# One layer step of a gated hybrid decoder on one core: six edits to a hand-ordered kernel (a bank's own signal, a norm moved, gates from a sum, transposes, constant matmuls, paired outputs)

## The chip, the cores and the metric

The kernel runs on one core of one Trainium2 chip. The metric is device time in microseconds for one launch. A run is also profiled; the profile's span is the time from the first to the last instruction of that execution.

## The reference

One step of one decoder layer in float32, for a prompt of 512 tokens and for 8 samples of one token each, model width 1024. All of it is computed for both.

```
h = rmsnorm(x, g_norm)
a_u, a_v, a_z, b_q, b_k, b_v, b_gd, b_z, c_q, c_z, gl = split(h @ w_in)
# A: spatial gating
vn    = layernorm(gelu(a_v), ln_v_g, ln_v_b)            # also an output, for the samples
out_a = gelu(a_u) * (tril(w_s) @ vn + b_s) * silu(a_z)
# B: gated linear attention, 4 heads, dk 128, dv 256
glog  = log_sigmoid(b_gd @ w_g_up + b_g) / 16            # b_gd = h @ (1024 x 16)
o, S  = chunked (prompt) or S = exp(g) S + k v, o = q S  (each sample, from its own state)
out_b = rmsnorm(o, gn_g) * silu(b_z)
# C: cross attention, 4 heads of 256, over 256 memory tokens
out_c = softmax(c_q k / 16) v * silu(c_z)                # samples: keys and values from a cache
x = x + sum_i(sigmoid(gl_i + b_gate_i) * (out_i @ w_branch_i)) @ w_out ;  y = rmsnorm(x, g_final)
```

## The kernel before

Activations are kept transposed: 128 channels on the partitions, 8 slices `k` of channels, and 520 columns (512 tokens, then the 8 samples). Every projection is an output of 1024 channels, cut in 8 tiles of 128. There are 17 of them, in the order of `NAMES`: QK, K, V, BV, BZ, CQ, GB, AZ, PB, AV, AU, GA, PA, CZ, GC, PC, OUT. A tile is named here by projection and number, AU6 is the seventh of AU.

Float32 accuracy comes from three products of split numbers: a weight `raw` is rounded to `w_hi` by ScalarE (`hi`, line 530), VectorE takes the remainder `w_lo` (`lo`, line 1390), and TensorE adds hi x lo, lo x hi and hi x hi over the 8 slices (`project`, line 1016). A tile is 48 such matmuls of some 260 columns. A pair of tiles is loaded by SP from DRAM to one of two slots of `raw`; the load of a pair waits for `split_done` of the pair two before.

There is no scheduler. Each engine runs a list written by hand: for each projection and each tile `c`, ScalarE does `hi` of the tile after next, the evacuation of the tile's bank in PSUM, and its hooks; VectorE does `lo` of the tile after next, `post`, and its hooks; TensorE does the projection and its hooks. So whatever stands in a hook of VectorE delays the next `lo` behind it.

The places that the change touches:

- **The start.** TensorE runs eight constant products of `ident` and `tri` (line 1315), then the transpose of the parameters (line 1317), and `x_turn` (line 1290), which transposes normalised x. ScalarE writes `h_hi` from the turned bank (line 551), VectorE `h_lo` (line 1821). The first two block columns of QK are made by `first_half` (line 1303).
- **K and V.** Between them TensorE makes the gates' low-rank input from `h_lo` and `h_hi` (line 1343), in four column groups `32 * i`.
- **BV and AV** are `HALVED`: the first 256 tokens are made as rows, two tiles together (line 994, for n = 0 and 1), the rest as columns (line 981). ScalarE's `evac_halves` copies both row banks out (lines 619 and 620) after both are done. `BEHIND` are the projections that follow, BZ and AU; their first tile uses the banks of the first half.
- **GB and AZ.** VectorE updates a sample's state of 4 x 128 x 256 (`sample_state`), one of four slots; POOL stores it and loads the state of the sample four later when `so_done` says that the slot was read. TensorE's `sample_out` (line 1143) multiplies the state with q, four heads in four column groups.
- **AV and AU.** VectorE's `decode_scores` (line 1709) multiplies cached keys with q. In AU, hooks of tiles 2 to 6 hold `layer_norm(n)`: rows 0 to 3 are blocks of 128 tokens in `tok`, row 4 the samples in `stok`. VectorE makes the statistics (lines 1677 and 1678), ScalarE the root (`ln_root`, line 797), VectorE the scaling (line 1681). For the token blocks POOL multiplies with `lng` and adds `lnb` (lines 467 and 468); for the samples VectorE does so (lines 1685 and 1686). The mix (line 1155, at GA's first tile) waits for all of them (`vn_ready`, `vns_ready`). AU's tile is evacuated to `stage` (line 668) and multiplied by VectorE (line 1410).
- **CZ0.** The decode attention's result `o_sb` is brought to channels on partitions by products with a selection `sel`, which POOL builds (line 1194), and copied to `ocs` (line 1528).

## Time and profile before

| | us |
|---|---|
| time of three runs, median (lowest to highest) | 871.77 (871.34 to 872.13) |
| time of the profiled execution | 871.54 |
| its span | 869.8 |
| TensorE matmuls busy | 854.6 (98%) |
| VectorE busy | 423.7 (49%) |
| ScalarE busy | 376.6 (43%) |
| POOL busy | 90.7 (10%) |
| DMA, mean over the span | 145 GB/s |

A row of a timeline gives start, duration, engine, line of the kernel, operation, output and inputs, shape, count, and in brackets how long the engine had been idle before it and what released it. Consecutive equal instructions are merged in one row. A float32 product of TensorE is recorded as two instructions, a transpose as one. `PEld` is the weight load of TensorE. The chain of waits is followed back from the last instruction.

### The profile page before, as it was taken

The page shows a single profiled execution, that of the slowest core. Times are in us where ns is not written, and L with a number is a line of the kernel's source. Part 1 is how long each engine was busy: PE and PEld are TensorE (multiplying, and loading weights), DVE is VectorE, ACT ScalarE, POOL GpSimd, SP SyncE. Part 2 cuts the span into 40 slices and gives each one's busy share as a digit, 9 for nine tenths or more (in the row PEclk, how much of TensorE's full clock was granted, in tenths as well). Part 3 has the DMA queues.
Part 4 walks back from the last instruction along what each step waited for, and adds up shares of the span by engine and source line. Part 5 has one row for each costly group of instructions (what it writes and reads, how often), then busy time and mean ns, then how long its engine had stood idle before and what let it go on. Part 6 is the DMA issues. An engine that isn't in the chain of part 4 may idle for free.

```text
span 869.8 us, 16391 instructions
## 1 busy us (share of the span) xinstructions
PE 854.6 (98%) x6975; PEld 826.9 (95%) x6975; DVE 423.7 (49%) x737; ACT 376.6 (43%) x596; POOL 90.7 (10%) x129
## 2 busy tenths in 40 slices
PE   7999999999999999999999999999999999999997
PEld 6999999999999999999999999999989999999995
DVE  5524542634554466323346778645343544445634
ACT  7534445246665442322232256433234544534424
POOL 1001000000000222101012147000110000000000
PEclk9999999999999999999999999999999999999999
DMA  8325743231322669523466951425563332252402
GB/s 294 80 87 170 250 146 97 93 104 49 97 99 75 217 212 348 175 67 106 164 215 213 323 194 49 148 98 194 194 243 98 97 123 72 98 189 79 145 2 99
DMA packets 86068, 126.11 MB, mean 145 GB/s; under 512 B 3058, under 2 KB 72736, under 8 KB 86000
## 3 DMA queue, kind: packets, MB, share of 16 engines
q1 hardware_dynamic: 72288, 76.58, 27.1%
q0 software_dynamic: 13616, 48.48, 15.7%
q8 instruction: 54, 0.88, 0.4%
q14 instruction: 14, 0.11, 0.0%
q10 hardware_dynamic: 96, 0.06, 0.0%
HBM read 112.91 MB, written 12.19 MB: 144 GB/s over the span
## 4 chain that ended last, share of the span: by engine, by line
PE 95%; DMA 1%; DVE 1%; ACT 1%; issue 1%; POOL 0%; ACTq 0%; DVEq 0%; POOLq 0%; SPq 0%
PE mm L1016 64%; PE mm L981 5%; PE mm L994 4%; PE mm L970 3%; PE mm L1303 2%; PE mm L1228 2%; DMA raw<-in_w_in_dram 1%; PE p L955 1%; PE p L957 1%; PE p L956 1%; PE mm L1249 1%; PE mm L1248 1%; PE mm L1247 1%; PE p L1155 1%; PE p L1185 1%; PE p L1129 1%
## 5 line engine op out<-in xcount | busy, mean ns | idle before, releaser
L1016 PE MATMUL mm<-h_lo,w_hi 128*128 128x260 f32 (+1 forms) x1088 | 223.3, 286 | 1.7 <-ACT tok L620 1.7
L1016 PE MATMUL mm<-h_hi,w_hi 128*128 128x260 f32 (+1 forms) x1088 | 219.0, 283 | 0.0
L1016 PE MATMUL mm<-h_hi,w_lo 128*128 128x260 f32 (+1 forms) x1088 | 218.5, 282 | 0.0
L1390 DVE TENSOR_TENSOR w_lo<-raw,w_hi 128x1024 fp32r<-128x1024 f32 x130 | 158.2, 1220 | 95.1 <-ACT w_hi L530 94.1
L1016 PEld LDWEIGHTS mm<-h_lo,w_hi 128*128 128x128 f32 x1088 | 167.9, 188 | 7.7 <-issue 6.0
L1016 PEld LDWEIGHTS mm<-h_hi,w_hi 128*128 128x128 f32 x1088 | 167.5, 188 | 0.0
L1016 PEld LDWEIGHTS mm<-h_hi,w_lo 128*128 128x128 f32 x1088 | 167.5, 188 | 0.0
L530 ACT ACTIVATE w_hi<-raw 128x1024 fp32r<-128x1024 f32 x130 | 135.9, 1053 | 7.5 <-issue 3.3
L1016 PE MATMUL mm<-x_lo,w_hi 128*128 128x260 f32 (+1 forms) x448 | 96.2, 284 | 0.0
L1016 PE MATMUL mm<-x_hi,w_hi 128*128 128x260 f32 (+1 forms) x448 | 95.3, 283 | 0.0
L1016 PE MATMUL mm<-x_hi,w_lo 128*128 128x260 f32 (+1 forms) x448 | 95.1, 282 | 0.0
L1016 PEld LDWEIGHTS mm<-x_lo,w_hi 128*128 128x128 f32 x448 | 71.2, 188 | 2.6 <-issue 2.6
L1016 PEld LDWEIGHTS mm<-x_hi,w_hi 128*128 128x128 f32 x448 | 71.2, 188 | 0.0
L1016 PEld LDWEIGHTS mm<-x_hi,w_lo 128*128 128x128 f32 x448 | 71.1, 188 | 0.0
L655 ACT ACTIVATE stage<-mm 128x520 f32<-128x520 f32 x24 | 14.5, 605 | 89.3 <-PE mm L1016 89.3
L671 ACT ACTIVATE gate<-mm,prm 128x520 f32<-128x520 f32 x24 | 16.7, 694 | 60.8 <-PE mm L1016 60.5
L994 PE MATMUL mm<-w_hi,h_lo 128*128 128x256 f32 x128 | 36.6, 286 | 0.0
L981 PE MATMUL mm<-h_lo,w_hi 128*128 128x264 f32 x128 | 36.6, 286 | 0.0
L981 PE MATMUL mm<-h_hi,w_lo 128*128 128x264 f32 x128 | 36.3, 283 | 0.0
L981 PE MATMUL mm<-h_hi,w_hi 128*128 128x264 f32 x128 | 36.3, 283 | 0.0
L994 PE MATMUL mm<-w_lo,h_hi 128*128 128x256 f32 x128 | 35.9, 281 | 0.0
L994 PE MATMUL mm<-w_hi,h_hi 128*128 128x256 f32 x128 | 35.9, 281 | 0.0
(358 smaller groups left out, 1361.2 us busy)
## 6 DMA issues: line engine op xcount, KB each, us to landing
raw<-in_w_in_dram SPq DMA_DIRECT2D x44, 1024.0 KB, 5.3
raw<-in_w_branch_dram SPq DMA_DIRECT2D x12, 1024.0 KB, 5.1
raw<-in_w_mem_kv_dram SPq DMA_DIRECT2D x8, 1024.0 KB, 5.6
gate<-in_cache_mem_k_dram POOLq DMA_DIRECT2D x16, 512.0 KB, 6.0
tok<-in_cache_mem_v_dram POOLq DMA_DIRECT2D x14, 512.0 KB, 5.8
tok<-in_state_gla_dram POOLq DMA_DIRECT2D x8, 512.0 KB, 6.8
out_dram<-tok POOLq DMA_DIRECT2D x8, 512.0 KB, 6.4
work<-scr_q POOLq DMA_DIRECT2D x8, 512.0 KB, 4.9
```

The lines of the kernel that those rows point to most:

```text
L530: A(w_hi[:, j], raw[:, j // 2, :, (j % 2) * P:(j % 2 + 1) * P], ACT.Copy).then_inc(hi_ready, 1)
L655: ins = A(st, src, ACT.Copy)
L671: ins = A(out3(gate), src, ACT.Sigmoid, bias=bg1[:, i * KT + c:i * KT + c + 1])
L955: MM(out, w[0], x[1], start=first_mm, stop=False)
L956: MM(out, w[1], x[0], start=False, stop=False)
L970: ins = MM(mm[:, j // 2, n, 0:2 * P], xp[:, k, ns], wp[:, j - 1:j + 1, k, :], start=(k == 0 and xp is x_lo), stop=(k == KT - 1 and xp is x ...
L981: ins = MM(mm[:, j % 2, 0, 0:TT - 256], wp[:, j, k, :], xp[:, k, 256:TT], start=(k == 0 and xp is h_lo), stop=(k == KT - 1 and wp is w_hi ...
L994: ins = MM(mm[:, n, 1, 0:2 * P], xp[:, k, n * P:(n + 1) * P], wp[:, j - 1:j + 1, k, :], start=(k == 0 and xp is h_lo), stop=(k == KT - 1 a ...
L1016: ins = MM(mm[:, j % 2, a, 0:c1 - c0], wp[:, j, k, :], xp[:, k, c0:c1], start=(k == 0 and wp is w_hi and xp is xl), stop=(k == KT - 1 and ...
L1228: ins = MM(o_bank[j % 4][:, 0:TT - 256], wp, xp[:, k, 256:TT], start=(k == 0 and xp is h_lo), stop=(k == KT - 1 and last))
L1303: ins = MM(mm[:, j % 2, j // 2, 0:c1 - c0], wp[:, j, k, :], xp[:, k, c0:c1], start=(k == 0 and xp is h_lo), stop=(k == KT - 1 and wp is w_ ...
L1390: V.tensor_tensor(w_lo[:, j], raw[:, j // 2, :, (j % 2) * P:(j % 2 + 1) * P], f32(w_hi[:, j]), ALU.subtract).then_inc(split_done, 1)
```

## The change

Six edits:

1. In BV and AV, TensorE signals the rows' first bank alone (`rows0_done`), ScalarE copies it out while the second is made and signals `rows0_out`, and the first tile of BZ and AU waits for that and for the first half's evacuation, no longer for the rows' second copy.
2. The samples' norm leaves `layer_norm`. Its statistics and root (`samples_norm`) stand at AU1, scaling, weight and bias (`samples_affine`, now two operations) at AU3, both with scalars of their own.
3. VectorE sums `h_hi` and `h_lo` into `h_sum`, one slice at each tile of K, and the gates are made from the sum, 32 products in place of 64.
4. The decode result is turned by eight transposes with `ident`, and four strided copies pick the columns; `sel` is gone.
5. The eight constant products at the start become twelve, four, two and four products of 128 columns from `state`, which VectorE fills with ones; they stand before and after the parameters' transpose and between the turns of x. The samples' input has a semaphore of its own, and ScalarE's second weight split moves from behind the eighth slice of `h_hi` to behind the sixth.
6. The samples' outputs are made two at a time, at GB4, GB6, AZ0 and AZ2, in place of one at each of GB3 to AZ2.

```diff
@@ evac_halves, ScalarE
+                cs = bass.ds((it * 4 + j - 1) * P, 2 * P)
+                act.wait_ge(sem("rows0_done"), HALVED.index(name) * KT // 2 + 2 * it + j // 2 + 1)
+                A(tok[:, 0, cs], mm[:, 0, 1, 0:2 * P], f).then_inc(sem("rows0_out"), 1)
                 act.wait_ge(prod_done, g + j + 1)
-                cs = bass.ds((it * 4 + j - 1) * P, 2 * P)
-                A(tok[:, 0, cs], mm[:, 0, 1, 0:2 * P], f)
                 A(tok[:, 1, cs], mm[:, 1, 1, 0:2 * P], f).then_inc(evac_done, 1)
@@ project, TensorE
-                wait(pe, evac_done, t if name in BEHIND and t == first(name) else t - 1)
+                wait(pe, evac_done, t - 1)
+                if name in BEHIND and t == first(name):
+                    pe.wait_ge(sem("rows0_out"), (BEHIND.index(name) + 1) * KT // 2)
@@ start and hooks, ScalarE
                 if k == 1:
                     hi(0, 0, 16)
-            hi(1, 1, 16)
+                if k == 5:
+                    hi(1, 1, 16)
...
-            act.wait_ge(sem("start_loaded"), 96)
+            act.wait_ge(sem("stok_loaded"), 16)
...
+                if name == "AU" and c == 1:
+                    act.wait_ge(sem("ln_mv"), 1)
+                    A(slstd, smv[:, 1:2], ACT.Sqrt, bias=eps_col[0:B, :]).then_inc(sem("ln_rt"), 1)
-                if name == "AU" and 2 <= c <= NT + 2:
+                if name == "AU" and 2 <= c < NT + 2:
                     ln_root(c - 2)
@@ hooks, TensorE
-                if name == "GB" and c >= 3:
-                    sample_out(c - 3)
-                if name == "AZ" and c <= 2:
-                    sample_out(c + 5)
+                if name == "GB" and c in (4, 6) or name == "AZ" and c in (0, 2):
+                    b = c - 4 if name == "GB" else c + 4
+                    sample_out(b)
+                    sample_out(b + 1)
@@ decode, TensorE
-                        ins = MM(p67[:, 0, k * B:(k + 1) * B], o_sb[:, k * P:(k + 1) * P], sel[:, k // 2, :, :],
-                                 start=(k == 0), stop=(k == KT - 1), skip_group_check=True)
+                        ins = TRP(p67_8[:, k, :], o_sb[:, k * P:(k + 1) * P], ident[:, :])
@@ start, TensorE
-            pe.wait_ge(sem("tri_ready"), 1)
-            for _ in range(8):
-                MM(mm[:, 0, 1, 0:2 * P], ident[:, :], tri[:, :, :], start=True, stop=True)
-            pe.wait_ge(sem("start_loaded"), 96)
+            def keep_busy(count):
+
+                for _ in range(count):
+                    MM(mm[:, 0, 1, 0:P], state[:, 0, 0:P], state[:, 0, 0:P], start=True, stop=True)
+
+            pe.wait_ge(sem("eps_ready"), 2)
+            keep_busy(12)
+            pe.wait_ge(sem("ident_ready"), 1)
+            pe.wait_ge(sem("start_loaded"), 80)
             TRP(prm_bank, prm_rows, ident[0:46, 0:46]).then_inc(sem("prm_T"), 1)
+            keep_busy(4)
...
                 if k == 4:
+                    keep_busy(2)
                     pe.wait_ge(sem("x_n"), 2)
                 x_turn(X_A + k)
+            keep_busy(4)
@@ gates, TensorE
-                        for xp in (h_lo, h_hi):
-                            for i in range(4):
-                                ins = MM(p67[32 * i:32 * i + RANK, 0, 0:Q4], gd_w[:, k, :], xp[:, k, i * Q4:(i + 1) * Q4].bitcast(F32),
...
+                        pe.wait_ge(sem("h_sum"), k + 1)
+                        for i in range(4):
+                            ins = MM(p67[32 * i:32 * i + RANK, 0, 0:Q4], gd_w[:, k, :], h_sum[:, k, i * Q4:(i + 1) * Q4],
@@ hooks, VectorE
+                if name == "K":
+                    if c == 0:
+                        dve.wait_ge(sem("memT_done"), KT)
+                    V.tensor_tensor(h_sum[:, c, :], f32(h_hi[:, c, :]), f32(h_lo[:, c, :]), ALU.add).then_inc(sem("h_sum"), 1)
...
                     if c == 1:
                         decode_scores((15,))
+                        samples_norm()
...
-                    if 2 <= c <= NT + 2:
+                    if 2 <= c < NT + 2:
                         layer_norm(c - 2)
+                    if c == 3:
+                        samples_affine()
...
-                    V.tensor_copy(ocs[:, :, :], p67[:, 0, 0:KT * B].rearrange("p (k b) -> p k b", b=B)).then_inc(sem("ocs_ready"), 1)
+                    for h in range(CH):
+
+                        turned = p67_8[:, 2 * h:2 * h + 2, :].rearrange("p d (j x) -> p d j x", x=32)[:, :, :, h:h + 8:4]
+                        ins = V.tensor_copy(ocs[:, 2 * h:2 * h + 2, :].rearrange("p d (g j) -> p d j g", j=4), turned)
+                    ins.then_inc(sem("ocs_ready"), 1)
@@ norms, VectorE (layer_norm keeps the token blocks alone)
+            def samples_norm():
+
+                dve.wait_ge(tr_used, TR["AV"] + KT)
+                dve.wait_ge(sem("stok_in"), 2 * KT)
+                for a in range(2):
+                    link(V.bn_stats(stats[0:B, a, :], stok[:, a * 512:(a + 1) * 512]))
+                V.bn_aggr(smv, stats[0:B, :, :]).then_inc(sem("ln_mv"), 1)
+                dve.wait_ge(sem("ln_rt"), 1)
+                link(V.reciprocal(slrst, slstd))
+
+            def samples_affine():
+
+                dve.wait_ge(sem("a_loaded"), 48)
+                link(V.scalar_tensor_tensor(out=stok[:, :], in0=stok[:, :], scalar=smv[:, 0:1], in1=lng[0:B, :],
+                                            op0=ALU.subtract, op1=ALU.mult))
+                V.scalar_tensor_tensor(out=stok[:, :], in0=stok[:, :], scalar=slrst, in1=lnb[0:B, :],
+                                       op0=ALU.mult, op1=ALU.add).then_inc(sem("vns_ready"), 1)
@@ VectorE's list begins
             V.memset(eps_col, EPS).then_inc(sem("eps_ready"), 1)
+            V.memset(state[:, 0, :], 1.0).then_inc(sem("eps_ready"), 1)
```

How the instructions stand at three of these places follows; the line numbers of the changed kernel differ from those of the kernel before. The start of TensorE's list, before:

```order
L1315 MATMUL mm<-tri,ident 128x256 [waits tri_ready,ident_ready]
L1315 MATMUL mm<-tri,ident 128x256 x7
L1317 MATMUL mm<-ident,stage 128x46 [waits start_loaded]
L1290 MATMUL p<-ident,mz 128x128 [waits x_n,x_n_act]
L1290 MATMUL p<-ident,mz 128x128 x7
```

And in the changed kernel:

```order
L1317 MATMUL mm<-state 128x128 [waits eps_ready]
L1317 MATMUL mm<-state 128x128 x11
L1323 MATMUL mm<-ident,stage 128x46 [waits start_loaded,ident_ready]
L1317 MATMUL mm<-state 128x128 x4
L1291 MATMUL p<-ident,mz 128x128 [waits x_n,x_n_act]
L1291 MATMUL p<-ident,mz 128x128 x7
L1317 MATMUL mm<-state 128x128 x2
```

The constants no longer wait for POOL, and there are some on both sides of the parameters' transpose. VectorE's list at AU6, before, from the last token block's norm in AU5 to the two splits at GA's beginning (`w_lo` is the split of a weight, `stok` are the samples' rows):

```order
L1681 TENSOR_SCALAR tok<-tok,small 128x1024 [waits dve_link]
L1390 TENSOR_TENSOR w_lo<-raw,w_hi 128x1024 [waits hi_ready]
L1410 TENSOR_TENSOR t<-t,stage 128x520 [waits evac_done]
L1504 SCALAR_TENSOR_TENSOR state<-p,tri 128x1024 [waits st_stored,wsT_done]
...
L1681 TENSOR_SCALAR stok<-stok,small 8x1024 [waits dve_link]
L1685 TENSOR_TENSOR stok<-stok,work 8x1024 [waits a_loaded,ln_norm]
L1686 TENSOR_TENSOR stok<-stok,work 8x1024 [waits dve_link]
L1390 TENSOR_TENSOR w_lo<-raw,w_hi 128x1024 [waits hi_ready]
```

The same engine in the changed kernel, AU1 and the split after it, and then AU3 and the split after it:

```order
L1705 BN_STATS small<-stok 8x6 [waits stok_in,tr_used]
L1705 BN_STATS small<-stok 8x6 [waits dve_link]
L1706 BN_AGGR small<-small 8x2 [waits dve_link]
L1708 RECIPROCAL small<-small 8x1 [waits ln_rt]
L1399 TENSOR_TENSOR w_lo<-raw,w_hi 128x1024 [waits hi_ready,dve_link]
...
L1698 TENSOR_SCALAR tok<-tok,small 128x1024 [waits dve_link]
L1713 SCALAR_TENSOR_TENSOR stok<-stok,small,work 8x1024 [waits a_loaded]
L1715 SCALAR_TENSOR_TENSOR stok<-stok,small,work 8x1024 [waits dve_link]
L1399 TENSOR_TENSOR w_lo<-raw,w_hi 128x1024 [waits hi_ready]
```

The samples' work stands ahead of the splits of AU4 and AU6 and no longer ahead of that of GA1. VectorE's list in K, before and in the changed kernel, two tiles each:

```order
L1401 COPY tok<-p 128x2x128 [waits tr_done]
L1390 TENSOR_TENSOR w_lo<-raw,w_hi 128x1024 [waits hi_ready]
L1401 COPY tok<-p 128x2x128 [waits tr_done]
L1390 TENSOR_TENSOR w_lo<-raw,w_hi 128x1024 [waits hi_ready]
L1401 COPY tok<-p 128x2x128 [waits tr_done]
```

```order
L1410 COPY tok<-p 128x2x128 [waits tr_done]
L1450 TENSOR_TENSOR gate<-h_hi,h_lo 128x520 [waits memT_done]
L1399 TENSOR_TENSOR w_lo<-raw,w_hi 128x1024 [waits hi_ready]
L1410 COPY tok<-p 128x2x128 [waits tr_done]
L1450 TENSOR_TENSOR gate<-h_hi,h_lo 128x520
```

A sum stands behind each copy, and the next split behind the sum.

## Rows read from the trace of the kernel before

**Rows 1.** The page: busy time, share of the span and instructions of each engine.

```profile
PE 854.6 (98%) x6975; PEld 826.9 (95%) x6975; DVE 423.7 (49%) x737; ACT 376.6 (43%) x596; POOL 90.7 (10%) x129
```

**Rows 2.** Who TensorE waited for: us in total, times, longest us.

```profile
PE mm L1016 <- ACT tok L620: 1.7, 2, 0.8
PE p L1155 <- issue: 1.5, 1, 1.5
```

**Rows 3.** Timeline of the start: start us, us, engine line op.

```profile
2.65 6.49 PE L1315 MATMUL mm<-tri,ident 128*128 128x256 f32 x16 [2.65 <-POOL tri L377]
...
8.02 0.88 DVE L1816 TENSOR_SCALAR mz<-mz,small 128x512 f32<-128x512 f32 x2
...
9.80 0.84 ACT L551 ACTIVATE h_hi<-p,prm 128x256 fp32r<-128x256 f32 x2 [0.22 <-PE p L1290]
...
10.53 1.06 ACT L530 ACTIVATE w_hi<-raw 128x1024 fp32r<-128x1024 f32 x1
...
13.78 1.05 ACT L551 ACTIVATE h_hi<-p,prm 128x256 fp32r<-128x256 f32 x2 [0.74 <-PE p L1290]
...
17.09 0.39 PE L1303 MATMUL mm<-h_lo,w_hi 128*128 128x256 f32 x1 [0.65 <-DVE w_lo L1390]
```

**Rows 4.** SP's two first weight loads, line 322: durations, first and last start, landing.

```profile
L322 SPq DMA_DIRECT2D raw<-in_w_in_dram x2: 427/518/608, 1.7 to 2.9; - x2
...
DMA to landing us min/median/max: 7.6/9.9/12.1
```

**Rows 5.** The chain of waits, in order of time: start us, us, what.

```profile
90.27 3.67 PE p L1343 x128
...
214.84 1.73 PE p L1129 x8
...
300.60 17.27 PE mm L1016 x144
317.87 0.55 PE p L1143 x8
318.42 5.94 PE mm L1016 x48
...
513.41 17.47 PE mm L1016 x144
...
655.03 1.68 PE p L1194 x16
...
665.41 0.87 PE p L1085 x8
```

**Rows 6.** Timeline of VectorE in BV, an operation with two inputs of 128x520.

```profile
166.57 0.68 DVE L1570 TENSOR_TENSOR gate<-gate 128x520 f32<-128x520 f32 x1
```

**Rows 7.** Timeline of VectorE at the end of K.

```profile
86.56 0.43 DVE L1401 COPY tok<-p 128x256 f32<-128x256 f32 x1 [1.51 <-PE p L1027]
...
89.62 0.42 DVE L1401 COPY tok<-p 128x256 f32<-128x256 f32 x1 [1.51 <-PE p L1027]
89.96 1.22 DVE L1390 TENSOR_TENSOR w_lo<-raw,w_hi 128x1024 fp32r<-128x1024 f32 x1
```

**Rows 8.** Timeline of VectorE and POOL in AU.

```profile
507.86 0.70 DVE L1410 TENSOR_TENSOR t<-t,stage 128x520 f32<-128x520 f32 x1 [2.54 <-ACT stage L668]
...
520.28 1.22 DVE L1390 TENSOR_TENSOR w_lo<-raw,w_hi 128x1024 fp32r<-128x1024 f32 x1
...
522.20 2.12 DVE L1410 TENSOR_TENSOR t<-t,stage 128x520 f32<-128x520 f32 x1 [0.69 <-ACT stage L668]
...
527.20 1.23 DVE L1390 TENSOR_TENSOR w_lo<-raw,w_hi 128x1024 fp32r<-128x1024 f32 x1
...
539.23 1.39 DVE L1677 BATCH_NORM_STATS2 small<-stok 8x6 f32<-8x512 f32 x2
...
542.23 1.21 DVE L1685 TENSOR_TENSOR stok<-stok,work 8x1024 f32<-8x1024 f32 x1
...
520.42 3.33 POOL L467 TENSOR_TENSOR tok<-tok,work 128x1024 f32<-128x1024 f32 x1 [0.97 <-DVE tok L1681]
```

More of the change, by code:

```diff
@@ L192, in bass_gated_parallel_step @@
         eps_col = small[:, 70:71]
+        smv, slstd, slrst = small[0:B, 71:73], small[0:B, 73:74], small[0:B, 74:75]
         def piece(base, at, shape):
@@ L209, in bass_gated_parallel_step @@
         Q4 = TT // 4
+        h_sum = gate
         eb = piece(work, 0, (BH, P))
@@ L252, in bass_gated_parallel_step @@
         sc = piece(work, 3744, (MT, B * CH))
-        sel = piece(work, 3808, (CH, 2, 4))
         o_sb = piece(work, 2 * D, (D,))
@@ L436, in _ @@
             pool.memset(pz.rearrange("p m b c -> p (m b c)"), 0.0).then_inc(sem("sel_ready"), 1)
-            link(pool.memset(sel.rearrange("p h g j -> p (h g j)"), 0.0))
-            pool.affine_select(out=sel, in_=sel, compare_op=ALU.not_equal, fill=1.0, base=0,
-                               pattern=[[-1, CH], [-4, 2], [-32, 4]], channel_multiplier=1).then_inc(sem("sel_ready"), 1)
             def load_q(b):
@@ L559, in _ @@
                 act.dma_start(prm_rows[at:at + rows.shape[0], :], rows).then_inc(sem("start_loaded"), 16)
-            act.dma_start(stok[:, :], x_sample.rearrange("b t d -> (b t) d")).then_inc(sem("start_loaded"), 16)
+            act.dma_start(stok[:, :], x_sample.rearrange("b t d -> (b t) d")).then_inc(sem("stok_loaded"), 16)
             act.wait_ge(sem("eps_ready"), 1)
@@ L794, in ln_root @@
             def ln_root(n):
-                rows = P if n < NT else B
-                act.wait_ge(sem("ln_mv"), n + 1)
-                A(lstd[0:rows, :], mv[0:rows, 1:2], ACT.Sqrt, bias=eps_col[0:rows, :]).then_inc(sem("ln_rt"), 1)
+                act.wait_ge(sem("ln_mv"), n + 2)
+                A(lstd, mv[:, 1:2], ACT.Sqrt, bias=eps_col[:, :]).then_inc(sem("ln_rt"), 1)
             def decode_exp():
@@ L995, in project_halves @@
                                      start=(k == 0 and xp is h_lo), stop=(k == KT - 1 and xp is h_hi and wp is w_hi))
+                    if n == 0:
+                        ins.then_inc(sem("rows0_done"), 1)
                 ins.then_inc(prod_done, 1)
@@ L1281, in out_project @@
                 out_rows(1, 1)
-            pe.wait_ge(sem("ident_ready"), 1)
             def x_turn(u):
@@ L1340, in _ @@
                     for k in range(KT):
-                        for xp in (h_lo, h_hi):
-                            for i in range(4):
-                                ins = MM(p67[32 * i:32 * i + RANK, 0, 0:Q4], gd_w[:, k, :], xp[:, k, i * Q4:(i + 1) * Q4].bitcast(F32),
-                                         start=(k == 0 and xp is h_lo), stop=(k == KT - 1 and xp is h_hi), skip_group_check=True)
+                        pe.wait_ge(sem("h_sum"), k + 1)
+                        for i in range(4):
+                            ins = MM(p67[32 * i:32 * i + RANK, 0, 0:Q4], gd_w[:, k, :], h_sum[:, k, i * Q4:(i + 1) * Q4],
+                                     start=(k == 0), stop=(k == KT - 1), skip_group_check=True)
                     ins.then_inc(sem("gd_done"), 1)
@@ L1671, in layer_norm @@
             def layer_norm(n):
[L1672 to L1675 removed]
+                rows = tok[:, n, :]
                 for a in range(2):
[L1677 to L1686 removed]
+                    link(V.bn_stats(stats[:, a, :], rows[:, a * 512:(a + 1) * 512]))
+                V.bn_aggr(mv, stats).then_inc(sem("ln_mv"), 1)
+                dve.wait_ge(sem("ln_rt"), n + 2)
+                link(V.reciprocal(lrst, lstd))
+                V.tensor_scalar(rows, rows, mv[:, 0:1], lrst, ALU.subtract, ALU.mult).then_inc(sem("ln_norm"), 1)
+            def samples_norm():
[12 more added lines that the diff above has]
+                                       op0=ALU.mult, op1=ALU.add).then_inc(sem("vns_ready"), 1)
             def mix(h):
```

15 lines of the change are left out of this document (removed).

## Prediction

> **What bounds the kernel now.** I read the page's busy times first. TensorE is busy for 854.6 of 869.8 us [rows 1], so the end moves only if TensorE gets less work or waits less. Its list of waits comes next: 1.7 us in two waits for the ScalarE copy of line 620, and 1.5 us in one wait before the mixing matmuls of line 1155 [rows 2]. The rest of its idle time lies in the start. Six stretches of the timeline then give the prices. The sum is made against the profiled execution, 871.54 us, which lies 0.23 us under the median of the three runs (871.77); I keep that execution as the base. About 0.2% (1.7 us) is what a measurement of this kernel can tell from no change.
>
> **1. Start.** Before, sixteen constant matmul records (eight fp32 products) keep TensorE until 9.1 us, though the first half of the token block's norm is scaled at 8.02 + 0.44 = 8.5 us (0.88 us is for both halves) [rows 3]. Afterwards the constants need only a short fill of `state` by VectorE, which can be done at about 1.3 us, instead of the triangle at 2.65. Each record takes 6.49 / 16 = 0.41 us for 256 columns, so 0.20 us for 128: 24 records end at about 6.2, the parameters' transpose comes then, and 8 more records end near 8.2. The turns of x start at 8.5 instead of 9.3. The parameters are in place long before, so ScalarE's first `h_hi` moves from 9.80 to about 9.0, and `w_hi` of tile 0 from 10.53 to about 9.7. Its weights were issued at 1.74 and land 7.6 us later, at 9.3 [rows 4], so they just allow this. Gain 0.8 us. Then tile 1: ScalarE idles 0.74 us before its seventh `h_hi` [rows 3]; the second weight split moves into that hole, while `h_hi` and `h_lo` of the last two slices come after it. That brings `w_lo` of tile 1 forward by another 0.5 us, and TensorE waits for exactly that at 17.09 [rows 3]. Together **-1.3 us**. If the constants end late or the weights land late it is 0; at most it is 1.3 plus the remaining 0.65 of idle time, -1.7 with what is hidden behind it. The samples' rows have a semaphore of their own, which only frees a wait that costs nothing today.
>
> **2. Gates from the sum.** The 128 records of line 1343 take 3.67 us [rows 5]; half of them take 1.8. For it VectorE makes eight sums of 128x520 inside K; the same shape, both inputs in SBUF, takes 0.68 us [rows 6]. A K tile takes TensorE 89.62 - 86.56 = 3.06 us by VectorE's copies, and VectorE 0.42 + 1.22 us [rows 7], so 0.68 more fits and the first six sums are covered. The last two are not: VectorE's copy of tile 6 starts at 89.62, the sum follows until 90.7, the next `w_lo` until 91.8, the copy of tile 7 until 92.2, the last sum until 92.9. TensorE, which begins the gates at 90.27, reaches the eighth slice at 91.8 and waits 1.1 us. It ends near 93.1 instead of 93.94: **-0.8 us**, between 0 (the sums are later still) and -1.8 (no wait). What queues behind the sums on VectorE, the splits of V, is next needed ten us later; SP's loads are issued 0.7 us later and still in time.
>
> **3. First bank of BZ and AU.** TensorE waits for that copy twice, before BZ and before AU, 1.7 us together, 0.85 each [rows 2]. Now the first bank is copied out while TensorE makes the second half of the rows, so both waits go: **-0.85 us at BZ** and as much at AU, which I book below.
>
> **4. Paired outputs of the samples.** Three plain tiles take 17.27 us, 5.76 each. With a sample's eight records between them the time from one to the next is 318.42 + 5.94 - 317.87 = 6.49 [rows 5], so an interruption costs 0.73 us. Four of the eight records run beside each other; at 0.216 us per record of 256 columns (1.73 us for eight that don't, line 1129 [rows 5]) the work itself is 2 x 0.216 = 0.43. The other 0.30 is the price of entering and leaving. Eight become four interruptions: 4 x 0.30 = **-1.2 us**. The states of samples 4 and 6 are now reloaded up to 4 us later, since their slots are free a tile later; I see no wait in it because they are used two tiles after that. Bounds: 0 (the gap is per record) and -1.5.
>
> **5. Samples' norm, in AU.** This is where the change can hurt. Removed: the wait of 1.5 us before the mix [rows 2], which VectorE causes by working on `stok` until 542.23 + 2 x 1.21 = 544.7 [rows 8]. Added earlier on VectorE: `samples_norm` after the last decode score (two statistics of 1.39 us together [rows 8], the aggregate, a wait for ScalarE's root, a reciprocal: some 2.2 us), and `samples_affine` behind the norm of the second row block (two operations of 1.21 us [rows 8]). The first falls into the 2.54 us that VectorE waits at 507.86 [rows 8], but ScalarE must load the Sqrt table and then the Gelu table again before it can evacuate AU's third tile, so I let the chain of norms start 0.5 us later. The second has no hole. VectorE's cycle per tile is 527.20 - 520.28 = 6.92 us there against 17.47 / 3 = 5.82 of TensorE [rows 5, 8], so it lives on its lead. And it meets POOL: `t<-t,stage` takes 2.12 us at 522.20 instead of 0.70, ending 0.6 us behind POOL's multiply (520.42 + 3.33 = 523.75); that multiply itself waited for `w_lo` to end [rows 8]. One holds the other up for a whole instruction, some 2.2 us of POOL work each.
> So: first affine operation 520.8 to 522.0. While the second waits for the first's result, POOL's multiply gets in, until 524.2. Second operation to 525.4, `w_lo` of AU6 behind it to 526.6. Before, AU6 began at 513.41 + 2 x 5.82 = 525.05 [rows 5]; with AU's gain of 0.85 it is due at 524.2 and stalls 2.4 us. The tiles behind it stall no more. Sum of this part: -0.85 - 1.5 + 2.45 = **+0.1 us**. Bounds: -2.35 if nothing collides, and +2.2 if POOL's addition also gets in ahead of `w_lo` (2.2 us more).
>
> **6. Decode transposes.** Sixteen records in 1.68 us become eight transposes; eight of these take 0.87 us [rows 5]. **-0.8 us.** The four small copies in place of one end long before VectorE's maximum of the scores, and POOL loses two small operations nobody waits for.
>
> Sum: -1.3 - 0.8 - 0.85 - 1.2 + 0.1 - 0.8 = -4.85; 871.54 - 4.85 = **866.7 us**.
>
> **Rivals.**
> (a) POOL first. At 525.4 both POOL's addition (asked for at 524.3) and `w_lo` want to go. The rows show POOL and VectorE each waiting for the other once, never a queue of two VectorE operations against a waiting POOL [rows 8], so this is nearly as likely as my case. Then `w_lo` of AU6 ends at 528.8, the stall is 4.6 us, part 5 is +2.2 and the time 868.8.
> The Trainium skill (SBUF — State Buffer, Who interferes with whom) says that issue order decides who blocks, and that the one that issued first holds the shared ports for its whole instruction. The 2.12 us row agrees with the blocking; taken literally the rule hands 525.4 to POOL and the time is (a)'s.
> (b) Light collision. POOL does not get in between the two affine operations; `w_lo` ends at 524.2, and only VectorE's 6.92 us cycle costs 1.2 us later. Part 5 is about -1: 865.7; without any stall 864.3.
> (c) One of the small edits does not pay: the start is set by the weights' landing, or the sums end later than I think. One of 0.8 to 1.3 us goes: 867.5 to 868.
> (d) Slower: TensorE stays at the lower clock level. The constants before ran at 0.41 us a record where the same shape later takes 0.216 [rows 3, 5], half pace, which is the 1.2 GHz level, though the clock row says full. The new stream has shorter records and two short gaps before the real matmuls (near 8.3 and 11.7). If it does not lift the clock, tile 0 starts at 12.1 at half pace and each two us cost one. The whole gain of 4.85 is gone if that lasts until 21.8; until 28 it costs 8.0 and gives 874.7. Against it: work begins 1.3 us earlier than before, and the gaps before 17.09 did no harm.
>
> **Numbers.** My case 0.40; (a) 0.28, (b) 0.19, (c) 0.10, (d) 0.03. My case's own range is 866.0 to 867.6. The range goes from 864.8, inside (b), to 869.2, above (a) with the start's gain a little smaller. Faster by over 0.2% (below 869.8): my case, (a) and (b) nearly whole and most of (c), 0.92. Within 0.2%: 0.05. Slower: (d), 0.03.
>
> **What would show it.** Start: first matmul of tile 0 near 12.1 and of tile 1 near 15.8. Gates: 64 records ending about 2.9 us after their start, with a wait of about 1.1 us for line 1450. No idle time before BZ and AU. Four groups of 16 sample records, each about 1.16 us. In AU: one wait of TensorE for `w_lo`, before the seventh tile, 2.4 us (4.6 in (a), none in (b)), VectorE's second `stok` operation longer than 3 us, and no wait before the mix. Decode: eight transposes in 0.87 us. I am wrong if TensorE waits in K or GB, if the AU wait lies at another tile, or if the start's matmuls have a pitch over 0.12 us.

## Result and profile after

The changed kernel takes 867.29 us (median of 4 runs, 866.57 to 868.86); the kernel before took 871.94 us on the same chip (median of 4, 871.34 to 872.13). The ratio is 0.995, with a 95% interval of 0.9937 to 0.9962: faster by 0.4 to 0.6%. The forecast was 866.7 us, between 864.8 and 869.2. One execution of the kernel before, beside the later runs, took 1695.61 us and is left out of their ratios.

The profiled execution is the slowest of the four, 868.86 us with a span of 866.6. It is compared with the profiled one of before (871.54, span 869.8), so the traces explain 3.2 us of span, and not the 4.65 of the medians.

The page, busy times, answering to [rows 1]:

```profile
PE 853.5 (98%) x6931; PEld 829.1 (96%) x6931; DVE 430.2 (50%) x748; ACT 377.3 (44%) x596; POOL 92.4 (11%) x127
```

TensorE lost 44 records and only 1.1 us of busy time, though the gates and the decode transposes alone save 2.6. Some other records must have become longer.

Who TensorE waited for in the changed kernel (us in total, times, longest), answering to [rows 2]:

```profile
PE mm L1020 <- DVE w_lo L1399: 2.0, 1, 2.0
PE mm L1323 <- DMA stage<-in_b_g_dram: 1.9, 1, 1.9
PE p L1352 <- DVE gate L1450: 0.8, 1, 0.8
```

The waits for ScalarE's row copy (0.85 twice) and the one before the mix (1.5) are gone. In their place stand 2.0 us before AU6, the forecast stall, 0.8 for the last sum, and 1.9 in the start for the parameters' load. One of 1.3 us stands ahead of the first constant product.

The chain of waits of the changed kernel (start, us, what), answering to [rows 5]:

```profile
17.00 5.93 PE mm L1304 x48
...
93.11 22.92 PE mm L970 x192
...
168.33 34.59 PE mm L1020 x288
...
298.69 23.03 PE mm L1020 x192
321.72 0.98 PE p L1147 x16
...
366.90 28.82 PE mm L1020 x240
...
485.62 17.30 PE mm L1020 x144
...
522.88 7.56 PE mm L1020 x48
...
542.85 0.89 PE p L1159 x8
...
652.85 0.87 PE p L1197 x8
656.55 5.74 PE mm L1020 x48
```

In the chain of before the same places start at 17.09, 93.94, 170.00, 300.60, 370.09, 489.65, 544.79 (the mix) and 659.64 (the matmuls behind the decode transposes). A subtraction gives a ledger of the span. "Forecast" is that of the same stretch:

| up to | before | after | gained in the stretch | forecast |
|---|---|---|---|---|
| tile 1 of QK | 17.09 | 17.00 | 0.09 | 1.3 |
| V (gates) | 93.94 | 93.11 | 0.74 | 0.8 |
| BZ | 170.00 | 168.33 | 0.84 | 0.85 |
| GB, first tiles | 300.60 | 298.69 | 0.24 | 0 |
| behind the last pair | 370.09 | 366.90 | 1.28 | 1.2 |
| AU | 489.65 | 485.62 | 0.84 | 0.85 |
| mix | 544.79 | 542.85 | -2.09 | -0.95 |
| behind the decode transposes | 659.64 | 656.55 | 1.15 | 0.8 |

The rest to the end is 0.1. Two lines are far off, the first and the one from AU to the mix.

**AU.** Timeline of VectorE and POOL in the changed kernel (start, us, engine line), answering to [rows 8]:

```profile
517.08 1.27 DVE L1713 SCALAR_TENSOR_TENSOR stok<-stok,small,work 8x1024 f32<-8x1024 f32 x1
518.38 3.31 DVE L1715 SCALAR_TENSOR_TENSOR stok<-stok,small,work 8x1024 f32<-8x1024 f32 x1
521.62 1.21 DVE L1399 TENSOR_TENSOR w_lo<-raw,w_hi 128x1024 fp32r<-128x1024 f32 x1
522.75 0.68 DVE L1419 TENSOR_TENSOR t<-t,stage 128x520 f32<-128x520 f32 x1
...
517.24 3.37 POOL L463 TENSOR_TENSOR tok<-tok,work 128x1024 f32<-128x1024 f32 x1 [0.97 <-DVE tok L1698]
520.69 4.99 POOL L464 TENSOR_TENSOR tok<-tok,work 128x1024 f32<-128x1024 f32 x1
```

POOL's multiply gets in between the two operations on `stok`, and the second one ends 1.1 us behind it, at 521.7: 3.31 us in place of 1.2. From there VectorE's two next operations with two inputs follow at their usual lengths (1.21, 0.68), and POOL's addition, which takes 2.73 us alone, is stretched to 4.99. So here VectorE's queue went ahead of the waiting POOL. Windows of the changed kernel around AU6 (us, busy of PE, PEld, DVE, ACT, POOL, then granted clock, DMA share, GB/s):

```profile
524.00:526.00 2.00, 2.00 (x11) 2.00 (x10) 1.53 (x5) 0.96 (x2) 1.68 (x1) 0.50 0.00 0
526.00:528.00 2.00, 2.00 (x15) 2.00 (x14) 1.55 (x2) 1.97 (x3) 1.54 (x1) 0.78 0.00 0
528.00:530.00 2.00, 2.00 (x19) 2.00 (x18) 1.76 (x1) 1.49 (x2) 1.92 (x2) 1.00 0.47 113
```

After 2.04 us of idle time TensorE resumes and soon falls to a granted clock of 0.50, its 1.2 GHz level, with 11 records in two us instead of 19. AU6 takes 7.56 us where a tile takes 5.82: 1.74 us behind the stall that no step of the forecast had.

**Start.** Timeline of TensorE and ScalarE in the start of the changed kernel, answering to [rows 3], and the window behind the parameters:

```profile
1.30 4.53 PE L1317 MATMUL mm<-state 128*128 128x128 f32 x24 [1.30 <-DVE state L1836]
7.69 0.23 PE L1323 MATMUL mm<-ident,stage 46*128 46x46 f32 x1 [1.86 <-DMA stage<-in_b_g_dram]
...
9.54 1.91 PE L1291 MATMUL p<-ident,mz 128*128 128x128 f32 x8
...
10.27 0.84 ACT L547 ACTIVATE h_hi<-p,prm 128x256 fp32r<-128x256 f32 x2 [2.10 <-PE p L1291]
```

```profile
8.40:11.00 2.60, 2.60 (x14) 2.60 (x13) 0.70 (x3) 0.73 (x2) 0.00 (x0) 0.50 1.03 396
```

The constants end at 5.8, the last parameter row lands at 7.55, and TensorE stands for 1.86 us. Then the clock falls to the same level, and the eight turns of x take 1.91 us instead of 1.09 and begin later than before. Tile 0 starts at 13.37 (forecast 12.1) and tile 1 at 17.00 (forecast 15.8). ScalarE's second weight split did move into its hole, and that alone kept tile 1 from being late.

### The profile page after: what moved, and what is told of

It is laid out like the page before. It is cut to its first block, busy times and chain, and to the rows that moved or that the text cites. A ratio compares the mean times of both kernels' runs of the same rounds, so it can differ in the third digit from the quotient of the medians.

```text
span 866.6 us, 16310 instructions
## 1 busy us (share of the span) xinstructions
PE 853.5 (98%) x6931; PEld 829.1 (96%) x6931; DVE 430.2 (50%) x748; ACT 377.3 (44%) x596; POOL 92.4 (11%) x127
## 4 chain that ended last, share of the span: by engine, by line
PE 95%; DVE 2%; ACT 1%; DMA 1%; issue 1%; ACTq 0%; DVEq 0%
PE mm L1020 63%; PE mm L981 5%; PE mm L994 5%; PE mm L970 3%; PE mm L1304 2%; PE mm L1230 2%; PE p L955 1%; PE p L957 1%; PE p L956 1%; PE mm L1251 1%; PE mm L1250 1%; PE mm L1249 1%; PE p L1189 1%; PE p L1159 1%; PE p L1133 1%; PE p L1130 1%
```

## Experiments

The question of the first four runs was what edit 2 is worth and whether the 2.0 us of idle time or something else slowed AU6. All times are medians. The first four runs, the next four and the last four were each made on another chip, where the kernel before took 871.62, 871.98 and 871.45 us: between these groups a difference of half a microsecond says little by itself, and the traces have to carry it. "AU to mix" is the difference of two starts in the chain: 55.14 us before, 57.23 after.

**The samples' norm back in AU5 and AU6** (the five other edits kept).

```diff
                     if c == 1:
                         decode_scores((15,))
-                        samples_norm()
...
-                    if 2 <= c < NT + 2:
+                    if 2 <= c <= NT + 2:
                         layer_norm(c - 2)
-                    if c == 3:
-                        samples_affine()
```

> The changed kernel with edit 2 alone undone: the samples' norm is again the fifth norm at AU6, the other five edits stay. My theory: in the changed kernel the second affine operation stood behind POOL's multiply (3.31 us), the split of AU6 ended at 522.8, TensorE waited 2.0 us and then ran AU6 at half pace (7.56 us against 5.82). With the norm back, no wait before AU6, AU6 in 5.8 us, and the wait of 1.5 us before the mix returns: from AU's start to the mix 55.1 us (changed kernel 57.2 in its profile). The time falls by about 0.5 us where the clock held and by 2.1 where it did not: near 866.3. Rival (the clock level falls by chance, not because of the wait): AU6 would be as likely to run slow here, and the time would not fall by more than 0.5.

865.99 us (865.66 to 867.18), ratio 0.9939 (0.9922 to 0.9955). AU to mix 54.90. No wait at AU6; the old one is back in the chain:

```profile
508.39 17.47 PE mm L1018 x144
...
538.26 1.51 issue
```

Edit 2 as it was made does not gain: taken out, the kernel's median is 1.3 us lower. The two ranges of times still overlap; in the traces, one execution each, the stretch is 54.90 against 57.23.

**The scale and shift at AU6 in place of AU3.**

```diff
-                    if c == 3:
+                    if c == 6:
                         samples_affine()
```

> The changed kernel with the samples' affine operations moved from AU3 to AU6 on VectorE, behind the mask product of the mixing weights; the statistics stay at AU1. My theory: neither AU6 nor the mix is waited for, 53.5 us from AU's start to the mix, no stretch at half pace in AU; 2.0 to 3.7 us below the changed kernel, near 865. Rival (the early statistics and the two extra table loads, not the affine part and POOL, are what delays AU6): a wait of 1 us or more before AU6 stays.

865.03 us (864.95 to 865.15), ratio 0.9925 (0.9909 to 0.9942): every run is below every run of the changed kernel. AU to mix 54.12, with a wait that was not expected:

```profile
508.23 17.47 PE mm L1020 x144
...
538.11 0.72 issue
538.83 1.13 PE p L1159 x8
```

What causes it stands in VectorE's timeline: the first operation on `stok` is stretched again, the second ends at 538.7, and the mix starts with it.

```profile
535.14 2.28 DVE L1713 SCALAR_TENSOR_TENSOR stok<-stok,small,work 8x1024 f32<-8x1024 f32 x1
537.46 1.27 DVE L1715 SCALAR_TENSOR_TENSOR stok<-stok,small,work 8x1024 f32<-8x1024 f32 x1
```

So the move of the norm is right and its place was not. The collision with POOL costs 1 us here and 2 us at AU3, and at AU6 no split that TensorE needs soon stands behind it; the price is the wait of 0.72 us.

**The two operations apart, at AU3 and AU4.**

```diff
                 if name == "AU":
+                    if c == 4:
+                        samples_affine(1)
...
                     if c == 3:
-                        samples_affine()
+                        samples_affine(0)
```

The second stands behind AU4's `post`, ahead of its norm.

> The changed kernel with the first affine operation at AU3 as it is, and the second at AU4, so that the split of AU6 stands between them. My theory: the gap between the two, in which VectorE waits for its own result, is what lets POOL in ahead of the split. With the split directly behind the first operation POOL comes after the split: no wait before AU6, the second operation costs its 1.2 us in the next cycle, so small waits at AU7 and GA0, some 1.3 us together, and 54.8 us from AU's start to the mix. If instead the amount of VectorE's work decides and not the gap, AU6 still waits 1 us or more.

866.28 us in one run, AU to mix 55.60 (expected 54.8). The stall at AU6 is gone, and two waits for AU's evacuation stand at AU7 and GA0, 1.8 us together (expected 1.3). VectorE, POOL, and who TensorE waited for:

```profile
518.56 0.68 DVE L1419 TENSOR_TENSOR t<-t,stage 128x520 f32<-128x520 f32 x1
519.17 3.41 DVE L1720 SCALAR_TENSOR_TENSOR stok<-stok,small,work 8x1024 f32<-8x1024 f32 x1
...
516.39 5.11 POOL L463 TENSOR_TENSOR tok<-tok,work 128x1024 f32<-128x1024 f32 x1 [0.96 <-DVE tok L1700]
...
PE mm L1020 <- ACT stage L666: 1.8, 2, 0.9
```

As expected, the split directly behind the first operation kept its 1.21 us. But the second operation is held for the same 2 us, although it stands directly behind `t`, with no gap in between. So the gap is not what alone lets POOL in. VectorE is late by as much as before, and the debt is only paid later, through ScalarE, which waits for the norm's statistics before its next evacuation.

**The old start** (constants behind the triangle again, the early weight split and edit 2 kept).

```diff
-            pe.wait_ge(sem("eps_ready"), 2)
-            keep_busy(12)
+            pe.wait_ge(sem("tri_ready"), 1)
+            for _ in range(8):
+                MM(mm[:, 0, 1, 0:2 * P], ident[:, :], tri[:, :, :], start=True, stop=True)
```

(and without the later `keep_busy`)

> The changed kernel with the old constants at the start: eight products of 256 columns after the triangle, none between the turns; the earlier second weight split stays. My theory: the start's gain of 1.3 did not come because the parameters land at 7.55 us, after the new constants have ended at 5.8, and TensorE's clock falls in that hole. With the old constants there is no hole: tile 0 at 12.9 as before, tile 1 at 16.6, all at full pace, clock mean 0.999 unless AU's wait lowers it. That is 0.4 us below the changed kernel's profile. Rival (the constants help when the clock holds, as in the changed kernel's fastest run): 0.5 to 1 us slower than the changed kernel in the median.

868.02 us (867.53 to 868.6), ratio 0.9959 (0.9945 to 0.9973), 0.7 us above the changed kernel, with ranges that overlap. Its profiled execution lost nothing in the start:

```profile
2.63 5.99 PE L1322 MATMUL mm<-tri,ident 128*128 128x256 f32 x16 [2.63 <-POOL tri L378]
...
16.05 0.39 PE L1304 MATMUL mm<-h_lo,w_hi 128*128 128x256 f32 x1
```

The same sixteen records took 6.49 us in the execution of before. With 5.99 they end at 8.6 and the turns start at 8.80. Earlier is hardly possible: with all constants ahead of the parameters (below) the turns wait for the scaled x and start at 8.79. So in this execution nothing is left for the new constants to gain. AU6 again takes 7.54 us behind a wait of 2.0 us, the second execution of two with that stall that shows the lower clock. That, and not the start, can be what sets this kernel above the fastest executions of the changed one: 865.6 us of span less the 1.7 that AU6 lost is 863.9, and those have 864.2 and 864.4.

**Is it the idle time that slows AU6?** Between AU5 and AU6 nine constant products of 128 columns in a free bank; nothing else of the changed kernel is touched, so VectorE is as late as in it.

```diff
+                if name == "AU" and c == 5:
+                    pe.wait_ge(evac_done, first("AU") + 5)
+                    for _ in range(9):
+                        MM(mm[:, 0, 1, 0:P], state[:, 0, 0:P], state[:, 0, 0:P], start=True, stop=True)
```

> The changed kernel with nine constant products of 128 columns (some 1.9 us) on TensorE between AU5 and AU6, where it waits 2.0 us for the split. Nothing else moves, the wait's end is set by VectorE. My theory: the half-pace stretch behind the wait comes from TensorE's idleness, so AU6 takes 5.8 us instead of 7.5 and the mix comes 1.7 us earlier than in the changed kernel's profile; AU to mix 55.5 us; median near 866.3. Rival (the stretch has another cause, such as power or chance): AU6 still takes 7.5 us in the profile.

866.41 us (866.19 to 866.56), ratio 0.9936 (0.9919 to 0.9954). Chain and window:

```profile
520.02 2.01 PE mm L1071 x18
522.06 6.01 PE mm L1020 x48
```

```profile
522.00:524.00 2.00, 1.97 (x17) 1.94 (x17) 1.93 (x5) 0.00 (x0) 2.00 (x1) 1.00 0.00 0
```

The stall is as long (the constants fill exactly 2.0 us), the clock stays at 1.00, and AU6 takes 6.01. AU to mix falls from 57.23 to 55.67. So the second half of the loss, some 1.6 us, came from the idle time through the clock, and not from VectorE, the banks or the loads. One profile alone could be a lucky execution. But all four executions here lie within 0.37 us, where those of the changed kernel are spread over 2.3, so the cause can be called shown.

**Sums earlier** (on the kernel with the scale and shift at AU6, as all that follow): three at K0, one at K1 to K5.

```diff
-                    V.tensor_tensor(h_sum[:, c, :], ...)
+                    for k in ((0, 1, 2), (3,), (4,), (5,), (6,), (7,), (), ())[c]:
+                        V.tensor_tensor(h_sum[:, k, :], ...)
```

> The kernel with the late affine operations (edit as in that run) and the sums of h one to two tiles earlier: three at K0, one at each of K1 to K5. My theory: in the changed kernel the gates wait 0.8 us for the last sum, which stands behind the copy of K7. With the sums done by K5 the gates run without a wait: 64 records in 1.85 us, V starts 0.8 to 1.1 us earlier relative to the end of K. Rival (VectorE's room in K is too small for three sums at K0): TensorE waits for a split in K, or the loads of V come later, and nothing is won.

868.28 us in one run, 3.2 above its base: a miss. In the chain V starts at 91.8 (base 92.1) although K lost 0.7 us by a split that three sums had delayed (TensorE waits 0.4 at 73.3). The rest is lost in V, where the third load landed 3 us later than in the base:

```profile
105.17 0.38 PE L970 MATMUL mm<-w_hi,x_lo 128*128 128x256 f32 x1 [1.73 <-DVE w_lo L1399]
...
106.00:108.00 2.00, 2.00 (x11) 2.00 (x10) 1.80 (x2) 0.35 (x1) 0.00 (x0) 0.50 0.69 196
```

An idle of 1.73 us, and again the level of 0.50 behind it, in a stage that has nothing to do with AU. It was issued at 91.07, in the base at 90.96, so the 3 us lie in the transfer and not in its issue. Why it took longer, this run can't say.

**The start's constants all ahead of the parameters** (eighteen products, none behind).

```diff
-            keep_busy(12)
+            keep_busy(18)
...
-            keep_busy(4)
+            keep_busy(0)
```

> The kernel with the late affine operations and eighteen constant products before the parameters' transpose, none behind it. The hole of 1.4 us before the parameters land is gone. My theory: the turns of x wait for nothing but the scaled x, which is ready at 8.5; tile 1 at about 15.9 instead of 16.1, at most 0.2 us gained where the clock holds, and the slow start of the changed kernel's profile (17.0) no longer occurs: the runs lie within 0.3 us. If the constants run cold to the end they last until 8.2, and nothing is lost. Rival (the hole costs nothing and more constants only delay): tile 1 later than 16.1.

865.04 us (864.97 to 865.17), ratio 0.9921 (0.9904 to 0.9939), the same as its base, and tile 1 at 16.03 against 16.07. The idle before the parameters is 0.71 instead of 1.36 us, but the base's own execution did not fall to the lower level either. So where the clock holds, constants behind the parameters bring nothing.

**Outputs one at a time again.**

```diff
-                if name == "GB" and c in (4, 6) or name == "AZ" and c in (0, 2):
...
+                if name == "GB" and c >= 3:
+                    sample_out(c - 3)
...
```

> The kernel with the late affine operations and the samples' outputs one at a time again (edit 6 undone). My theory: an interruption of the stream costs 0.30 us beyond its matmuls; eight instead of four cost 1.2 us, so the stretch from GB's fourth tile to AZ's fourth is 1.2 us longer and the time 866.2. Rival (the price is per record, or the later reload of states hides something): less than 0.4 us.

866.5 us in one run. From 297.83 the chain needs 69.48 us to the matmuls behind the last output, against 68.22 in its base. A single output there (the pair of the changed kernel is in the chain above):

```profile
315.10 0.55 PE p L1147 x8
315.64 5.94 PE mm L1020 x48
```

Eight of these against four pairs are 1.26 us; the forecast was 1.2.

**Four parts alone or shifted**, each against the kernel with the scale and shift at AU6 (865.03 us):

```diff
# the second weight split behind the eighth slice again
-                if k == 5:
-                    hi(1, 1, 16)
+            hi(1, 1, 16)
```

> The kernel with the samples' scale and shift at AU6 (e2_affine_late: 865.0 us, tile 1 of the start at 16.07), with one thing undone: ScalarE rounds the start's second weights behind the eighth slice again, as before the change, while the constant products keep their new places. The run with the old constants already reached tile 1 at 16.05. Theory (the split's move carries the start's gain, the constants' places nothing): tile 1 at 17.0 and 865.9. Rival (both moves are needed or neither, the start is set by the loads): tile 1 at 16.1 and 865.0.

865.77 us (865.7 to 866.41), ratio 0.9936 (0.9919 to 0.9953). The wait of before is back, and tile 1 is 0.59 us later than in the base:

```profile
16.66 0.39 PE L1303 MATMUL mm<-h_lo,w_hi 128*128 128x256 f32 x1 [0.64 <-DVE w_lo L1398]
```

The median is 0.74 higher. The split's move is worth 0.6 us by the trace (expected 0.9, forecast 0.5); the rest is less than what the groups of runs differ by.

```diff
# gates from h_lo and h_hi, no sums
-                        pe.wait_ge(sem("h_sum"), k + 1)
...
+                        for xp in (h_lo, h_hi):
```

> The same base (e2_affine_late, 865.0 us) with the gates' products from h_lo and h_hi again, 128 records, and no sums on VectorE. Theory (the sum's edit is worth its forecast of 0.8, of which 0.83 is still lost to the wait for the last sum): V's first product 0.75 later than the 92.1 of the base, no wait in the gates, 865.8. Rival (the weights' splits on VectorE, freed of eight operations of 0.69, come earlier and give some of it back in K or V): 865.2 to 865.5.

865.83 us (865.51 to 866.16), ratio 0.9934 (0.9917 to 0.9951).

```profile
89.83 3.67 PE p L1352 x128
93.50 22.92 PE mm L970 x192
```

V starts at 93.50 and in the base at 92.19: 1.31 later, of which 0.57 is this execution's start (tile 1 at 16.64), so 0.74. Its start had 1.66 us of idle time before the parameters and the clock at 0.50 behind it.

```diff
# scale at AU3, shift at AU6
+                    if c == 3:
+                        samples_affine(0)
                     if c == 6:
-                        samples_affine()
+                        samples_affine(1)
```

> The same base (e2_affine_late, 865.0 us, from AU's start to the mix 54.12 with a wait of 0.72 before the mix) with the two operations of the samples' scale and shift apart: the first, 1.27 us, at AU3, the second at AU6. Theory (the wait before the mix is the last norm's, and VectorE is late by the length of these two operations): the wait before the mix is gone or under 0.2, AU to mix 53.6, 864.5. Rival (VectorE's operation of AU6 still asks for the port behind GpSimd's multiply and takes over 3 us): the wait stays at 0.7 or grows, 865.0 to 865.6.

865.61 us (865.31 to 866.37), ratio 0.9931 (0.9914 to 0.9947): not better than the base. AU to mix is 54.47 us, 0.35 more than there. The profiled execution, 866.37 us, is the slowest of the four: it stood for 2.03 us before the parameters, the clock fell behind that, and tile 1 started at 17.26. The wait before the mix is gone, and one of 0.8 us for AU's evacuation has taken its place. The one operation at AU3 shifted VectorE against POOL, so that now the split collides, and `t` directly behind it too:

```profile
523.25 3.40 DVE L1399 TENSOR_TENSOR w_lo<-raw,w_hi 128x1024 fp32r<-128x1024 f32 x1
526.57 2.88 DVE L1419 TENSOR_TENSOR t<-t,stage 128x520 f32<-128x520 f32 x1
...
522.71 2.86 POOL L464 TENSOR_TENSOR tok<-tok,work 128x1024 f32<-128x1024 f32 x1
525.53 3.36 POOL L463 TENSOR_TENSOR tok<-tok,work 128x1024 f32<-128x1024 f32 x1
...
PE mm L1020 <- ACT stage L666: 0.8, 1, 0.8
```

```diff
# sums one slice ahead: one at K0, two at K1, one at K2 to K6
-                    V.tensor_tensor(h_sum[:, c, :], ...)
+                    for k in ((0,), (1, 2), (3,), (4,), (5,), (6,), (7,), ())[c]:
+                        V.tensor_tensor(h_sum[:, k, :], ...)
```

> The same base (e2_affine_late, 865.0 us) with VectorE's eight sums one slice ahead of their turn: one at K0, two at K1, one at each of K2 to K6, none at K7. With three at K0 the one execution lost 0.4 at K1, gained 1.0 in the gates, and then lost 1.7 in V to weights that landed late, and 1.5 more at half the clock level behind that idle. Theory (that late load was chance, and only the wait for the last sum, 0.83, depends on the sums' places): no wait in the gates, V's first product 0.7 earlier, 864.3. Rival (gates that end earlier bring V to weights that are not there): a wait of 1 us or more in V, and 866 to 868.

864.15 us (864.03 to 865.21), ratio 0.9919 (0.9902 to 0.9935), the lowest median of all.

```profile
89.21 1.90 PE p L1352 x64
91.10 22.92 PE mm L970 x192
```

No wait in the gates, none in K, and none in V. Gates that end earlier therefore do not of themselves run into missing weights; of the three sums at K0 it follows only that they delay a split. Three of its four runs lie below every run of its base, which was measured on another chip; the intervals of the two ratios overlap widely, and it is V's start, 1.09 us earlier, that carries the reading. It beats both kernels: 864.15 against 867.29 and 871.45.

## Why the prediction was right, and where it was not

**The time** was forecast 0.6 us below the median. The steps did not all hold: two terms were each wrong by more than 1 us, both towards too fast. The profiled execution is 2.2 us above the forecast. What brings the median near it are 0.24 us behind each wait that went, and, as far as the granted clocks tell, executions in which the clock fell less often than in the profiled one (below). That it came so near is in part luck.

**2, gates.** Right: 64 records in 0.74 us less (forecast 0.8), with a wait of 0.83 for line 1450 (forecast 1.1). Undone, the edit costs 0.74 again.

**3, first bank.** Right at both places, 0.84 each. The chain gained another 0.24 behind each that I had not booked.

**4, pairs.** Right: 1.28 and, by the experiment, 1.26, against 1.2; the price of entering and leaving is 0.3 us per interruption. No wait for a reloaded state appeared.

**6, decode transposes.** Right: 0.87 us in the chain for 1.68.

**5, samples' norm.** The mechanism was right down to the place: one stall, at the seventh tile, from POOL's multiply between the two operations, 2.04 us (forecast 2.45), no wait before the mix. What failed is the sentence that the stall costs its own length. The term +2.45 should have been 2.04 + 1.74 = 3.8, for the clock level behind it; the run with constant products in the gap shows the second part. From AU to the mix the change lost 2.09 us where +0.95 was forecast. With the -0.85 before AU, part 5 was +1.25 and not +0.1.

**1, start.** The term of -1.3 failed; it was -0.09 in the profiled execution. Its second half was right: the weight split is worth 0.6. Its first half, 0.8 for the turns of x, assumed that "the parameters are in place long before", and no row had shown when they land, because the old constants ended later than they did. The transpose that waits for them started at 7.2 to 7.9 in the executions seen: they land after TensorE's first constants have ended, not long before. In executions without the fall of the clock tile 1 comes at 16.03 to 16.24, a gain of 0.85 to 1.06, and the run with the old constants reached 16.05 too. So what the new constants bring is at most what the old ones lose when they are slow (6.49 against 5.99 us), and with the fall tile 1 comes 0.6 to 1.2 us later (16.64, 17.00 and 17.26 in three executions). Rival (c) had this in a milder form; rival (d) had the clock, but for the wrong reason: not records too short to lift it, but an idle in front of them.

**(a) POOL first** fell in this kernel. It supposed that the waiting POOL gets the port when VectorE's second operation ends, which also is what the rule of the Trainium skill (SBUF — State Buffer, Who interferes with whom: the operation that issued first holds the shared ports) gives when it is taken literally. The trace disagrees here: POOL's addition is recorded from 520.69, `w_lo` from 521.62, and `w_lo` took 1.21 us, its usual length. But that is no rule the other way. In two experiments an operation directly behind another was held for POOL's multiply (`stok` 3.41 us with the two operations apart, `t` 2.88 us with scale at AU3 and shift at AU6). The prediction's choice between its own case and (a) was right for this place, and what decides it stays open. **(b)** fell with the stall. **(d)** as a whole fell: the full level was back by 11.5.

**How the median can be lower than the profiled execution.** The mean granted clock of the four executions was 0.995, 0.999, 0.997 and 0.999, their spans 866.6, 864.2, 865.6 and 864.4. Without the two falls (0.9 and 1.7 us) the profiled span would be 864.0. That fits executions with both, one or none of them; it is an inference, since only the first was profiled.

## What to carry to other kernels

A gap in TensorE's work has two prices, its length and what the clock does behind it, and the second was nearly as large as the first here (1.74 behind 2.04 us). A forecast that trades two short waits for one long one should count it, and where a gap can't be closed, constant matmuls in it are a cheap probe and a partial cure. When VectorE and POOL both work on two SBUF inputs, an operation of VectorE can be held for a whole instruction of POOL, and standing directly behind another one does not reliably protect it (1.21 and 0.68 us here, 3.41 and 2.88 us in two experiments): put the extra work where the splits behind it are not due, and look for the next operation that slides into the collision when one is moved.

Before a fill is shortened, find out when the load lands that it had been hiding.

## What was not expected of the hardware

- TensorE at the lower level after short gaps. It fell to 0.50 behind idle times of 2.04 and 2.0 us (AU6), 1.73 us (V) and 1.86, 2.03 and 1.66 us (start). It stayed at 1.00 behind 1.51 us (before the mix), 1.40, 1.36, 1.04 and less. A fall cost 0.6 to 1.2 us in the start and 1.5 to 1.7 later. In the start the gap differs from execution to execution because the same 24 constant records took 4.39 to 5.49 us: the three executions that fell are the three in which they were quickest (4.39, 4.41 and 4.53 us). Constants that run fast end too soon and leave the hole that they were to fill.
- A gap costs some 0.25 us beyond its length even when the clock holds. Without the gaps of 0.85 us the 288 records of BZ took 34.59 us in place of 34.84, AU's first three tiles 17.30 in place of 17.54, the first group of the mix 0.89 in place of 1.13; and V started 1.09 us earlier when the wait of 0.83 in the gates was gone.
- Small operations of 8 partitions and 1024 columns take as long as those of 128 partitions (1.27 against 1.21 us), and hold up or are held up by POOL just the same (3.31 us).

- How long a held instruction takes. It ends its own work behind the end of the other one: POOL's stretched addition 2.25 us behind `t` (525.68 and 523.43), its stretched multiply 2.26 us behind `t` with the two operations apart (521.50 and 519.24), VectorE's held operations on `stok` 1.1 us behind POOL's multiply. So POOL was most likely held through both `w_lo` and `t`, and its recorded length is mostly waiting.

What stays open: why VectorE's queue goes first in one place and POOL in another; why the third load of V took 3 us longer in the run with three sums at K0; and how often, in unprofiled executions, the level falls behind a gap of 1.4 to 2.0 us.
